# Softmax attentions with the normalisation moved from a VectorE pass over the probabilities into the TensorE product that turns them

## What is computed

```python
def attend(qb, k, v):                              # hybrid block, 4 heads of 64, up to 768 keys
    s = jnp.einsum("bhgqd,bhkd->bhgqk", qb, k).astype(jnp.float32) * (HEAD_DIM ** -0.5)
    p = jax.nn.softmax(s, axis=-1).astype(v.dtype)
    return jnp.einsum("bhgqk,bhkd->bhgqd", p, v)

# window attention: 8 heads of 64, a band of up to 384 keys, and a sink in the denominator
    m = jnp.maximum(jnp.max(scores, axis=-1, keepdims=True), sk)
    p = jnp.exp(scores - m)
    denom = jnp.sum(p, axis=-1, keepdims=True) + jnp.exp(sk - m)
    o = jnp.einsum('bnhgqk,bnkhd->bnqhgd', p / denom, vw)

# cross attention: 4 heads of 256, 256 keys
    p = jax.nn.softmax(jnp.einsum('bqhd,bkhd->bhqk', q, k) * (CROSS_HEAD_DIM ** -0.5), axis=-1)
    o = jnp.einsum('bhqk,bkhd->bqhd', p, v).reshape(b, s, D_MODEL).astype(h.dtype)
```

## Time and profile before

| | |
|---|---|
| median of three runs | 1808.47 us |
| the runs | 1807.28, 1808.47, 1814.75 us |
| span of the profiled execution, first to last instruction | 1813.4 us |
| own time of the profiled execution | not listed apart; of the three runs only 1814.75 us is longer than the span |
| PE busy | 1680.7 us (93%) |
| DVE busy | 844.6 us (47%) |
| ACT busy | 710.2 us (39%) |
| POOL busy | 591.9 us (33%) |
| mean granted TensorE clock | 0.978 of full |

### The profile page before, as it was taken

The page is one execution under the profiler, slowest core; times in us unless marked ns, Lnnn a source line. Parts: engine busy times, 40 slices in busy tenths (PEclk is TensorE's granted clock), DMA queues, the critical chain, the costliest instruction groups (busy, mean ns, idle before and its releaser), DMA issues.

```text
span 1813.4 us, 32533 instructions
## 1 busy us (share of the span) xinstructions
PE 1680.7 (93%) x13634; PEld 1367.6 (75%) x13634; DVE 844.6 (47%) x1539; ACT 710.2 (39%) x1101; POOL 591.9 (33%) x312
## 2 busy tenths in 40 slices
PE   6999999988989989989999988789899899999997
PEld 3787888866878767758878757687688688888886
DVE  3101275476340356476757567565424445544113
ACT  5325213254352624354644967013523432222222
POOL 1122323193313221453024303222235244444443
PEclk8999999999999989999999998999999999999999
DMA  8444311310122211402522210001121133223332
GB/s 330 172 141 143 114 49 48 114 39 12 59 94 71 68 59 60 140 1 93 176 96 90 82 36 2 4 3 47 50 90 47 47 104 104 94 94 104 96 111 73
DMA packets 43865, 152.23 MB, mean 84 GB/s; under 512 B 4560, under 2 KB 7888, under 8 KB 43600
## 3 DMA queue, kind: packets, MB, share of 16 engines
q1 hardware_dynamic: 40176, 140.76, 23.5%
q10 hardware_dynamic: 3552, 9.47, 1.4%
HBM read 146.02 MB, written 4.19 MB: 83 GB/s over the span
## 4 chain that ended last, share of the span: by engine, by line
PE 78%; DVE 11%; ACT 6%; issue 4%; DMA 1%; POOL 0%; SPq 0%; DVEq 0%; ACTq 0%
PE wide_ps L1956 53%; PE wide_ps L2013 4%; DVE xn L1427 1%; PE wide_ps L2583 1%; PE wide_ps L2031 1%; PE wide_ps L2254 1%; PE pair_ps L2072 1%; PE duo_ps L2053 1%; DVE xn L1680 1%; DMA ring<-weights 1%; PE duo_ps L2729 1%; ACT xn L909 1%; PE wide_ps L2710 1%; PE wide_ps L1978 1%; DVE proj L1345 1%
## 5 line engine op out<-in xcount | busy, mean ns | idle before, releaser
L592 POOL TENSOR_TENSOR ring_r<-ring,scratch_r 128x1024 fp32r<-128x1024 f32 x168 | 411.0, 2447 | 941.3 <-ACT scratch_r L770 868.2
L1956 PE MATMUL wide_ps<-xn_r,scratch_r 128*128 128x512 f32 x1272 | 468.7, 368 | 0.0
L1956 PE MATMUL wide_ps<-work_r,scratch_r 128*128 128x512 f32 (+1 forms) x1109 | 425.1, 383 | 8.2 <-POOL ring_r L592 6.3
L1956 PE MATMUL wide_ps<-work_r,ring_r 128*128 128x512 f32 (+1 forms) x1109 | 409.3, 369 | 0.0
L770 ACT ACTIVATE scratch_r<-ring 128x1024 fp32r<-128x1024 f32 x190 | 200.9, 1058 | 507.2 <-PE wide_ps L1956 444.7
L1956 PEld LDWEIGHTS wide_ps<-xn_r,scratch_r 128*128 128x128 f32 x1272 | 240.4, 189 | 43.9 <-issue 5.1
L1956 PEld LDWEIGHTS wide_ps<-work_r,scratch_r 128*128 128x128 f32 x1109 | 209.5, 189 | 54.8 <-issue 12.0
L1956 PEld LDWEIGHTS wide_ps<-work_r,ring_r 128*128 128x128 f32 x1109 | 209.1, 189 | 36.4
L1956 PE MATMUL wide_ps<-proj_r,scratch_r 128*128 128x512 f32 x634 | 211.9, 379 | 0.0
L1956 PEld LDWEIGHTS wide_ps<-proj_r,scratch_r 128*128 128x128 f32 x634 | 119.0, 188 | 22.7 <-ACT xn L754 0.4
L754 ACT ACTIVATE proj<-wide_ps 128x512 f32<-128x512 f32 (+2 forms) x86 | 56.6, 658 | 201.0 <-PE wide_ps L1956 193.4
(11 more groups left out here) (459 smaller groups left out, 2979.6 us busy)
## 6 DMA issues: line engine op xcount, KB each, us to landing
ring<-weights SPq DMA_DIRECT2D x254, 512.0 KB, 3.5
h<-tokens SPq DMA_DIRECT2D x4, 768.0 KB, 11.2
h<-tokens ACTq DMA_DIRECT2D x1, 3072.0 KB, 10.2
out<-h ACTq DMA_DIRECT2D x1, 2048.0 KB, 7.3
h<-out ACTq DMA_DIRECT2D x1, 2048.0 KB, 9.4
out<-h SPq DMA_DIRECT2D x16, 128.0 KB, 1.7
proj<-weights SPq DMA_DIRECT2D x2, 512.0 KB, 15.0
h<-mem ACTq DMA_DIRECT2D x1, 1024.0 KB, 12.8
```

The lines of the kernel that those rows point to most:

```text
L592: pool.tensor_tensor(as_r(wt), wt, as_r(w_lead(m)).bitcast(F32), ALU.subtract).then_inc(w_split, 1)
L1956: last = pe.matmul(bank[:, a:b], wt[:, cols], as_r(x[:, a:b]), start=n == 0 and p == 0, stop=n == len(k_order) - 1 and p == 2)
```

## The change

The DVE pass over the probabilities goes, in all three attentions. In its place DVE multiplies a stretch of the constant tile (the identity, and one column behind it, 129 columns in all) by the same reciprocal, into one of four slots of a new tile `diagonal_of`. PE's transposes against the identity become fp32 matmuls with the unnormalised probabilities as the stationary operand, as before, and the diagonal as the moving one: the product turns a block of 128 columns and multiplies each query's column by its reciprocal in one. The scores, maxima, exponentials, copies and value products stay, and so do the number and the order of the program's operations on every engine; a slot of `diagonal_of` is guarded by two added waits of DVE on PE's turns (`w_pt_ps`, `c_pt_ps`), while the hybrid block has none.

```diff
+        diagonal_of = sb("diagonal_of", [P, 4, P + 2])
...
+        ident_wide = const[:, CONST_COLS["ident"][0]:CONST_COLS["ident"][0] + P + 1]
...
                 for n in range(1, len(pairs) + 3):
                     p = ATT0[ly] + n
                     if n <= len(pairs):
-                        a, b = keys_of(pairs[n - 1][1])
                         for r in range(2):
                             m = 2 * p - 2 + r
                             one = slice(m % 4, m % 4 + 1)
-                            prob = pair_probs(p - 1)[:, r * (b - a):(r + 1) * (b - a)]
                             dve.wait_ge(at_exp, m + 1)
                             link(dve.reciprocal(row_inv[:, one], row_sum[:, one]))
-                            dve.tensor_scalar(prob, prob, row_inv[:, one], None, ALU.mult).then_inc(at_p, 1)
+                            dve.tensor_scalar(diagonal_of[:, m % 4, 0:P + 1], ident_wide, row_inv[:, one], None, ALU.mult).then_inc(at_p, 1)
...
                 if 1 <= n <= len(WIN):
                     m = n - 1
-                    a, b, _, _ = window_keys(WIN[m][1])
                     dve.wait_ge(w_exp, 3 * m + 3)
+                    if m >= 2:
+                        dve.wait_ge(w_pt_ps, m - 1)
                     link(dve.tensor_tensor(win_stat(row_sum2, m), win_stat(row_sum2, m), win_stat(sink_e, m), ALU.add))
                     link(dve.reciprocal(win_stat(row_inv2, m), win_stat(row_sum2, m)))
                     for r in range(2):
-                        one = slice(2 * (m % 2) + r, 2 * (m % 2) + r + 1)
-                        p = probs(m)[:, r * (b - a):(r + 1) * (b - a)]
-                        dve.tensor_scalar(p, p, row_inv2[:, one], None, ALU.mult).then_inc(w_p, 1)
+                        k = 2 * (m % 2) + r
+                        dve.tensor_scalar(diagonal_of[:, k, 0:P + 1], ident_wide, row_inv2[:, k:k + 1], None, ALU.mult).then_inc(w_p, 1)
...
                     link(dve.reciprocal(row_inv2[:, one], row_sum2[:, one]))
-                    dve.tensor_scalar(probs(n)[:, 0:CTX], probs(n)[:, 0:CTX], row_inv2[:, one], None, ALU.mult).then_inc(c_p, 1)
+                    if n >= 4:
+                        dve.wait_ge(c_pt_ps, n - 3)
+                    dve.tensor_scalar(diagonal_of[:, n % 4, 0:P + 1], ident_wide, row_inv2[:, one], None, ALU.mult).then_inc(c_p, 1)
...
                             for t in range(4):
-                                last = pe.transpose(turn_bank(g)[:, t * P:(t + 1) * P],
-                                                    pair_probs(p - 1)[:, 512 * q + t * P:512 * q + (t + 1) * P], cst["ident"])
+                                r = (4 * q + t) // (2 * ATT_TURNS[p - 1])
+                                last = pe.matmul(turn_bank(g)[:, t * P:(t + 1) * P],
+                                                 pair_probs(p - 1)[:, 512 * q + t * P:512 * q + (t + 1) * P],
+                                                 diagonal_of[:, (2 * p - 2 + r) % 4, 0:P], start=True, stop=True)
...
-                            last = pe.transpose(win_turned[:, r, t * P:(t + 1) * P], probs(m)[:, at:at + P], cst["ident"])
+                            last = pe.matmul(win_turned[:, r, t * P:(t + 1) * P], probs(m)[:, at:at + P],
+                                             diagonal_of[:, 2 * (m % 2) + r, 0:P], start=True, stop=True)
...
-                        last = pe.transpose(twin(n)[:, t * P:(t + 1) * P], probs(n)[:, t * P:(t + 1) * P], cst["ident"])
+                        last = pe.matmul(twin(n)[:, t * P:(t + 1) * P], probs(n)[:, t * P:(t + 1) * P],
+                                         diagonal_of[:, n % 4, 0:P], start=True, stop=True)
```

## The result

| | before | after |
|---|---|---|
| median, runs of one comparison | 1810.18 us (5 runs) | 1824.57 us (5 runs, 1821.90 to 1830.67) |
| ratio to before | | 1.0069, 95% interval 1.0052 to 1.0086 |
| profiled execution: own time, span | span 1813.4 us | 1823.06 us, span 1821.0 us |

The change makes the kernel slower. The ratio is 12.5 us of 1810, with an interval of 9.4 to 15.6; the forecast said +14.4. The same kernel was run once more, in another comparison and with six runs (the last experiment): 1.0071, interval 1.0053 to 1.0089.

The account below looks back on a forecast made before the run. PE, busy 93% of the span with 78% of the chain, was taken as the bound, with DVE also near it in the hybrid and window attentions. Hybrid 9.0 + window 2.0 + cross 3.4 = +14.4 on 1808.47: 1822.9 us, range 1811 to 1830.

Parts of the forecast that it names:

- the case forecast: All attentions: the multiply still waits for POOL and a tile costs 0.223 us; +14.4 us, range +9 to +21, chance 0.56.
- Price of a tile: PE's turns in all attentions: a tile goes from 0.107 to 0.223 us, 320 tiles adding +37 us of PE work.
- The diagonal: DVE's 129-column multiply in all attentions: 0.29 us alone, and near 1.8 us beside POOL, for which it still waits.
- The rival of the slip: Hybrid block: the odd, narrow multiply does not wait for POOL; sum +8.4 us, down to +4 at full clock; chance 0.30.
- Undisturbed pairs: Hybrid block, six pairs of 768 keys: PE becomes the bound, 5.21 to 5.93 us each, +4.4 us for six.
- Layer 0: Hybrid block's layer 0, beside undisturbed pairs: first pair +0.4, four disturbed iterations -1.0, one later pair +0.2, last three +1.8.
- Layer 1: Hybrid block's layer 1, beside undisturbed pairs: first two iterations +1.2, the 2.29 us wait's iteration +0.4, last turns +1.65.
- the one with the 2.29 us wait keeps its wait, +0.4: Layer 1 iteration where PE waits 2.29 us: the wait stays after the change, costing +0.4 us.
- its first two iterations +1.2: Start of the hybrid block's layer 1: its first two iterations get longer by +1.2 us.
- Window: Window attention: +2.0 us, bounds 0 and +6; four units at 10.83 us, +0.5 over three groups, the rest at the edges.
- PE takes over: Window attention: PE replaces DVE as the bound, so four units take 10.83 us, +0.15.
- Cross: Cross attention, 16 units of PE alone: 32 tiles at 0.115 us, less 0.3 for a DVE wait, +3.4 us.

Follow-up runs that it names:

- e1: Changed kernel with DVE's old passes put back and PE's fp32 product taken against the plain identity: 1821.93 us, ratio 1.0065.
- e4: Changed kernel, the hybrid block's multiply reading a gapped identity copy (three rows of 44) and writing 132 columns in one run: 1816.35 us, ratio 1.0025.
- e3: Changed kernel with the diagonal's multiply 128 columns wide in place of 129: 1822.36 us, ratio 1.0060.
- e6: Kernel before with the change in the cross attention alone: 1812.99 us, ratio 1.0019.
- e9: Kernel before with the change in the window attention alone: 1813.64 us, ratio 1.0011.
- e2: Changed kernel with PE's old transposes put back, diagonals still written, normalisation left out of the output: 1803.75 us, ratio 0.9961.
- e7: Kernel before with the product for five hybrid pairs only, their diagonals written by the multiply of e4: 1802.61 us, ratio 0.9961.
- e8: e7 with POOL doing the second head's pass in the window attention: 1803.72 us, ratio 0.9960 to the kernel before.
- e5: Kernel before with the change in the hybrid block alone: 1817.78 us, ratio 1.0032.

## Why the prediction was right, and where it was not

The time is 1824.57 against 1822.9 forecast, inside the range, and the case forecast is the one that came. Its steps:

- **Price of a tile: right.** 416, 160 and 64 instructions, 0.22 us a tile at full clock in the cross attention, 0.44 for its two (a little more elsewhere: 3.00 us for twelve in the hybrid block). The factor of two that the row of the values product gave holds, and e1 shows the same two instructions with the plain identity. The Trainium skill's four ("TensorE: Matmul & The Clock Gate", Terms) does not hold: 0.22 against 0.11 us.
- **The diagonal: right.** 284 ns in the window, for 0.29 taken; and it waits for POOL, up to 2.20 us. The rival of the slip is thereby out for this kernel; e4 shows what it would have been: ratio 1.0025, some 4.5 us (2.4 to 6.9), where I had worked out 8.4, and down to 4 with a full clock. The Trainium skill's rule on the two-port mode ("Advanced Engine Details and Errata", VectorE Performance Modes: sizes both even, or both odd and equal) agrees three times: 129 columns wait (after), 128 columns wait (e3), and unlike outer sizes, 3 rows of 44 against 132, don't (e4).
- **Undisturbed pairs: right.** 5.95 us for the 5.93 forecast, and no ACT wait before the third turn.
- **Layer 0: right to 0.3 us.** First iteration +0.3 (forecast +0.4); the stretch of four disturbed ones 23.84 to 22.92, or -0.9 (-1.0); the one behind the third undisturbed pair +0.2 (+0.2); the last ones +1.9 (+1.8). In all +3.8, for +3.6.
- **Layer 1: too high.** Forecast +5.4, measured +2.3 (+1.4 against e6 and e9). The step that failed is "the one with the 2.29 us wait keeps its wait, +0.4": it came at -1.6. The step before it, "its first two iterations +1.2", came at -0.2. Two rows of before (PE, then DVE):

```profile
772.40 2.93 PE L2254 MATMUL wide_ps<-proj 64*128 64x512 f32 x8 [1.53 <-ACT xn L909]
...
780.37 2.50 DVE L1427 TENSOR_SCALAR xn<-xn,small 128x768 f32<-128x768 f32 x1
```

and the timeline of after (DVE, then POOL) what came in its place:

```profile
779.80 2.20 DVE L1427 TENSOR_SCALAR diagonal_of<-const_sb,small 128x129 f32<-128x129 f32 x1
782.10 2.20 DVE L1427 TENSOR_SCALAR diagonal_of<-const_sb,small 128x129 f32<-128x129 f32 x1
781.88 2.34 POOL L594 TENSOR_TENSOR ring_r<-ring,scratch_r 128x1024 fp32r<-128x1024 f32 x1
```

The first two iterations are the clock's doing. The scores at 772.40 ran at half the clock, 2.93 us where 1.56 is usual, and that iteration took 6.68 us; in after, at full clock, it takes 5.95. The step itself was sound: with the same code and no such spell (e6 and e9, 10.58 and 10.57 us for the two) the change costs 11.82 - 10.57 = +1.2 us, as forecast. The longer turns did not keep the clock up, as far as is shown: behind the same waits of 0.34 and 1.53 us it stayed full in e2, e6, e7, e8 and e9, and fell in before alone.

The wait for POOL is the real miss. Both multiplies still wait for it, to 782.00 and 784.30. But before, DVE began the pass of r = 0 at 780.37, 1.29 us after PE began the scores (779.08), and PE stood through its wait; in after the multiply of r = 0 begins at 779.80, 1.43 us ahead of the scores (781.23), and is over when turn 0 comes at 782.72. PE waits only for the second one, 0.47 us in place of 2.29 and 0.23. It takes both halves of the change. With PE as the bound and the long passes kept (PE's timeline of e1) the waits are

```profile
784.65 1.16 PE L2280 MATMUL pair_ps<-const_sb,xn 128*128 128x128 f32 x8 [0.16 <-DVE xn L1429]
787.28 2.05 PE L2280 MATMUL pair_ps<-const_sb,xn 128*128 128x128 f32 x16 [1.47 <-DVE xn L1429]
```

and with the short multiply but the old turns (e2) they are 0.33 and 1.65 us. The old code has 1.35 and 1.96 there (e9, above). So each half alone takes some 1.3 to 1.7 us off the 3.3, and the two together leave 0.47.
- **Window: the sum held, a term did not.** Alone it measures 1.0011, or 2.0 us, the forecast's number, but the interval runs from -0.5 to +4.5, and the profiles give 0.3 to 3.9: the agreement shows little. The period of four units was to be 10.83 us and is 11.33 (PE's timeline of after):

```profile
1081.17 1.61 PE L2525 MATMUL pair_ps<-diagonal_of,xn 128*128 128x128 f32 x12 [0.28 <-DVE diagonal_of L1694]
...
1083.30 0.70 PE L2513 MATMUL wide_ps<-proj 64*128 64x256 f32 x4
...
1092.51 1.61 PE L2525 MATMUL pair_ps<-diagonal_of,xn 128*128 128x128 f32 x12 [0.27 <-DVE diagonal_of L1694]
...
1094.63 0.70 PE L2513 MATMUL wide_ps<-proj 64*128 64x256 f32 x4
```

I had said "PE takes over". It does for three units of four, and the fourth still waits 0.28 us (0.35 with the 0.07) for DVE: a sum over a group is no bound when the units differ in length. The remaining 0.15 us is PE's own. Three groups at +0.65 each in place of +0.15 are 1.5 us more. At the edges I had expected some of the cost back from the clock, and by these two profiles it came: the last but one turn ran at half clock before (six tiles in 1.54 us, at 1100.07) and at full clock after (six tiles in 1.58 us, now as twelve instructions, at 1106.44). But in e5 and e6, with the old code and the same wait of 1.12 us ahead of it, it ran at full clock as well (0.88 us), so that the change kept the clock up is not shown.
- **Cross: right to 0.5.** +2.95 for +3.4.

By the stretches the hybrid block cost 6.1 us, where the forecast had 9.0, and the sum is 10.6, where it had 14.4. The time by the ratio lies nearer to the forecast, 12.5 and 12.9 us, but part of this agreement is luck. Layer 1 was taken too high by 3 us or more. Against that, the profiled execution of before had a long window stretch, so the two profiles show less than the 12.5 us that the ratio gives; the lengths in e5, e6 and e9 would give those 12.5. Some 2 us between stretches and ratios stay unplaced, inside the interval.

## What to carry to other kernels

Before work is moved from a loaded engine to another loaded one, count the gaps that the move will fill: each half of this change, measured by itself, read as -8.4 and +10.9 us, but most of the saving lay in the gaps that the cost closed. Where one of many like steps is held by a neighbour (here POOL), apply the trade to those steps alone, chosen from the timeline: five pairs of twenty turned +12.5 us into -7. And a wait is not to be carried over as a constant when the change makes the waiting engine the bound: what it waits for can then run ahead of it, the more so when its own step is shorter. Last, a spell of the clock can fall into the very stretch that is priced: a second profile of the same code shows it (e9 for layer 1).

## What the runs showed that I had not expected

- An fp32 multiply on DVE with source rows of 44 and a destination in one piece never waited for POOL: 349 to 352 ns in forty cases, where the plain form took 286 to 2204. For 60 ns each it removes waits of up to 2 us.
- A stretch's length hangs on TensorE's clock even where the code is the same: the window attention took 48.87 to 51.22 us. The spells at 1.2 GHz came behind gaps of PE (1.53 us in layer 1 of before, 1.35 and 1.96 in e6 and e9), but not behind every one: after the same 1.53 us the clock stayed full in five other runs. With fewer gaps (e7) it stayed at 1.00 in both hybrid stretches.
- POOL takes 0.92 and 1.24 us for a multiply of 128x256 and 128x384 fp32, 2.6 and 3 times what DVE takes (0.35 and 0.42).
